# Expert loop of a decoder layer: token rows turned by VectorE in squares of 32 instead of by TensorE

## The chip, the cores and the metric

The kernel runs on one core of a Trainium2 chip. The metric is the device time of the program in microseconds (us). Times of whole runs are the median of three; the profile is of one more execution.

## The reference

One layer of a decoder: three attention groups on 512 tokens of width 1024, an output projection, and then the part that concerns us, a mixture of 32 experts with the four best experts for each token:

```
h = RMSNorm(x)
logits = h @ w_router + b_router            # 32 experts
top_v, top_e = top_k(logits, 4); gates = softmax(top_v)
for every expert e, on the tokens that chose it (padded blocks):
    gu   = h @ w_gate_up[e] + b_gate_up[e]  # 1024 -> 2048, gate = even, up = odd columns
    gate = min(gu[0::2], 7);  up = clip(gu[1::2], -7, 7)
    act  = (up + 1) * gate * sigmoid(1.702 * gate)
    y    = act @ w_down[e] + b_down[e]      # 1024 -> 1024
x = x + sum over the token's 4 experts of gate * y;  out = RMSNorm(x)
```

All inputs are float32, and all 32 experts' weights (12 MB each) are read from HBM.

## The kernel before, in words

The first 330 us or so compute the attention part, the router and a table that gives, for each block of up to 128 rows, the expert, the tokens and the gates. The rest is a loop over blocks. Here there are 33 blocks, 0 to 32: block 0 is done ahead of the loop, blocks 1 to 31 run through a loop body, and block 32 is the last, with a tail behind it.

**Arithmetic.** A float32 product is computed as three products of rounded parts: every operand is split into a high part (ScalarE, an `activation` copy to fp32r) and a low part (VectorE, the original minus the high part). `three` (lines 1296 to 1298) issues high x high, high x low and low x high into one PSUM bank.

**Weights.** A block needs twelve tiles of 1 MB: eight of gate and up (`gate_up`, rows k*128 to k*128+127 of the expert's matrix, 2048 columns) and four of down. SyncE loads each into one of six slots of `raw` (L448 and L455) once VectorE is done with the tile six before it. ScalarE makes the high part in one of four slots of `w_hi` (`hi`, L598) once TensorE has used the tile four before it (`half_used`); VectorE makes the low part in `w_lo` (`lo`, L859) once the high part is there; TensorE multiplies once the low part is there (`lo_ready`), twelve matmuls of 512 columns for each tile.

**Order within a block b.** It is written out by hand, engine by engine:

- TensorE (`one_block`): gate and up tiles 0 to 2, eight transposes of the previous block's activation (`turn_acts`, L1583), tiles 3 to 7, four bias matmuls (`gu_bias`, L1569), eight transposes of the next block's token rows (`turn_rows`, L1576), then the four down tiles of the previous block's activation.
- VectorE: low parts of tiles 4 to 6; the low parts of the turned activation in two halves (`turn_act`, L1174); low parts of tile 7 and of down tiles 0, 1 and 2; `clamp` (L1186, L1188); down tile 3; the low parts of the turned token rows in two halves (`turn_x`, L1169); `activate` (L1196); low parts of tiles 0 to 3 of the next block.
- ScalarE: the high parts in the same order, with the two turned operands (L751, L746), the sigmoid (L757) and the scaled output rows (`y_out`, L764) between them.
- GpSimd: an indirect DMA that gathers the next block's 128 token rows of 4 KB from `normed_rows` in HBM into `h_row` (`gather`, L539), four small DMAs for the biases (L571), and an indirect DMA that scatters the output rows (`scatter`, L564).

The eight transposes of `turn_rows` put token rows, features on the partitions, into PSUM banks 6 and 7; so do those of `turn_acts` for the activation. All of it is ordered by semaphores alone.

Of the kernel before, what the change touches and what calls it, by code (L numbers as in the profile page):

```python
# [10 lines left out]
I32 = mybir.dt.int32  # L11
# [37 lines left out]
N_CONST = C_FIRST + 2 * NT  # L49
# [16 lines left out]
def constants():  # L66
    c = np.zeros((P, N_CONST), np.float32)
    p = np.arange(P)
    c[:, C_IDENT:C_IDENT + P] = np.eye(P)
    c[:, C_TRI:C_TRI + P] = p[:, None] < p[None, :]  # L70
    c[:, C_ONES:C_ONES + P] = 1.0
    c[:, C_IOTA:C_IOTA + P] = p[None, :]
    for t in range(NT):
        c[:, C_TOK + t] = TOPK * (t * P + p) - NO_ROW
        c[:, C_FIRST + 2 * t] = t * P + p - NO_ROW
    c[:, C_ROWMOD] = p % E
    return c
# [14 lines left out]
def hymba_layer(nc, x, mem, attn_norm_g, mem_norm_g, w_in, diff_lambda_qk, diff_subln_g, w_mem_kv,  # L92
# [5 lines left out]
    h_dram = nc.dram_tensor("normed_rows", (S, D), F32).ap()  # L98
    y_dram = nc.dram_tensor("expert_rows", (TOPK * S, D), F32).ap()
# [11 lines left out]
    gu_dram = w_gate_up[0].rearrange("e (k p) n -> e p k n", p=P)  # L111
    dn_dram = w_down[0].rearrange("e (k p) n -> e p k n", p=P)

    with ExitStack() as ctx:
# [28 lines left out]
        exp_psum = psum[5][:, 2 * MAX_BLOCKS:3 * MAX_BLOCKS]  # L143
        pair_turn = turn_psum[:, :].rearrange("p (j s) -> p j s", j=2)
# [88 lines left out]
        gate_t, exp_f = (tabs[:, i, :] for i in (1, 2))  # L233
# [5 lines left out]
        idx_scatter = F[:, 15001:15002].bitcast(I32)  # L239

# [5 lines left out]
        last_tok = nrm[:, 0, 8:9]  # L246
        h_row = F[:, 4096:5120]
        act = F[:, 5120:6144]
# [44 lines left out]
        xtp_done, xhi_ready, xlo_ready = sem("xtp_done"), sem("xhi_ready"), sem("xlo_ready")  # L293
        atp_done, ahi_ready, alo_ready = sem("atp_done"), sem("ahi_ready"), sem("alo_ready")
# [126 lines left out]
        def _(sp):  # L421
# [22 lines left out]
            def gate_up(e, k, i, free=None):  # L444

                if free is not None:
                    sp.wait_ge(lo_ready, free)
                sp.dma_start(raw[:, i % 6, :].rearrange("p (e n) -> p e n", e=1),  # L448
                             gu_dram[bass.ds(e, 1), :, k, :]
                             .rearrange("e p n -> p e n")).then_inc(raw_in[i % 6], 16)  # L450
# [23 lines left out]
            with sp.Fori(1, loops + 1) as b:  # L474
                before, e = (sp.value_load(exp_i[0:1, bass.ds(b + i, 1)], min_val=0, max_val=E - 1)
                             for i in (-1, 0))
                for k in range(GU):
                    gate_up(e, k, GU + k, b * 12 + (7 + k))
                for j in range(DN):
                    down(before, j, 2 * GU + j, b * 12 + (7 + GU + j))  # L480
# [28 lines left out]
        def _(pool):  # L509
# [16 lines left out]
            for g in range(2):  # L526
                for i in range(2):
                    r0 = (2 * g + i) * E
                    pool.dma_start(bias_in[r0:r0 + E, :].rearrange("e (c n) -> e c n", c=2),
                                   b_gate_up[0].rearrange("e (c g n) -> g e c n", c=2, g=2)[g]).then_inc(bias_in_s, 16)  # L530
            pool.wait_ge(exp_ready, 1)
            loops = pool.value_load(loops_i[0:1, :], min_val=E - 1, max_val=MAX_LOOPS)

            def gather(column, n):
                n = n if isinstance(n, int) else pool.snap(n)
                pool.tensor_copy(idx_gather, tok_i[:, column]).then_inc(idx_ready, 1)  # L536
                pool.wait_ge(idx_ready, n)
                pool.sem_inc(gather_go, 1)
                pool.indirect_dma_start(h_row, None, h_dram,  # L539
                                        bass.IndirectOffsetOnAxis(idx_gather, 0),  # L540
                                        bounds_check=S - 1, oob_is_err=False).then_inc(h_in, 16)

            pool.wait_ge(tab_ready, 1)
            gather(slice(1, 2), 1)
# [28 lines left out]

            pool.wait_ge(bias_saved, 16)
# [5 lines left out]
            pool.wait_ge(xtp_done, loops + 1)  # L580
            bias_of_block(loops)
            scatter(loops - 1, loops * 2 + 1)
            pool.wait_ge(y_sent, loops * 16 + 32)
            pool.wait_ge(h_in, loops * 16)
# [3 lines left out]
        def _(a):  # L588
# [159 lines left out]

            def turn_act(q, n, into=ha):
# [19 lines left out]
            a.sem_inc(ahi_ready, 1)  # L769
# [20 lines left out]
            with a.Fori(1, loops) as b:  # L790
                for i in range(4, 7):
                    hi_m(GU + i, b)
                turn_act(0, b)
                turn_act(1, b)
                for i in range(7, 12):
                    hi_m(GU + i, b)
                sigmoid(b + 1)
                turn_x(0, b + 2)
                turn_x(1, b + 2)
                for i in range(12, 16):  # L800
                    hi_m(GU + i, b)
                y_out(b * 12 + (16 + GU), bass.ds(b - 1, 1), b * 16 + 16)
# [3 lines left out]
            turn_act(0, b)  # L806
            turn_act(1, b)
# [23 lines left out]
        def _(v):  # L831
# [306 lines left out]
            def read_table():  # L1138

                v.wait_ge(tab_in, 1)  # L1140
                link(v.tensor_scalar(y_row_i, tab_psum[:, 0:MAX_BLOCKS], float(NO_ROW), None, ALU.add))
                link(v.tensor_copy(gate_t, tab_psum[:, MAX_BLOCKS:2 * MAX_BLOCKS]))
                v.tensor_scalar(tok_i, y_row_i, 2, None, ALU.arith_shift_right).then_inc(tab_ready, 1)  # L1143
                v.wait_ge(tab_ready, 1)

# [21 lines left out]
            def turn_x(q, n, high=hx, low=lx):  # L1167
                v.wait_ge(xhi_ready, n)
                v.tensor_tensor(low[:, 4 * q:4 * q + 4, :], psum[6 + q][:, :].rearrange("p (k s) -> p k s", k=4),  # L1169
                                high[:, 4 * q:4 * q + 4, :].bitcast(F32), ALU.subtract).then_inc(xlo_ready, 1)  # L1170

# [38 lines left out]
            for i in range(4, GU):  # L1210
                lo_m(i)
            split_biases()
# [17 lines left out]
            with v.Fori(1, loops) as b:  # L1230
                for i in range(4, 7):
                    lo_m(GU + i, b)
                turn_act(0, b * 2)
                turn_act(1, b * 2 + 1)
                for i in range(7, 11):
                    lo_m(GU + i, b)
                clamp(b + 1)
                lo_m(GU + 11, b)
                turn_x(0, b * 2 + 3)
                turn_x(1, b * 2 + 4)  # L1240
                activate(b + 1, b)
                for i in range(12, 16):
                    lo_m(GU + i, b)
# [3 lines left out]
            turn_act(0, b * 2)  # L1247
            turn_act(1, b * 2 + 1)
# [7 lines left out]
            turn_act(0, b * 2 + 2, hx, lx)  # L1256
            turn_act(1, b * 2 + 3, hx, lx)
# [35 lines left out]
        def _(pe):  # L1293
# [243 lines left out]

            def half_in(i, b):
# [33 lines left out]
            def turn_rows(n_h):  # L1572

                pe.wait_ge(h_in, n_h)
                for k in range(KT):
                    ins = pe.transpose(psum[6 + k // 4][:, k % 4 * P:(k % 4 + 1) * P],  # L1576
                                       h_row[:, k * P:(k + 1) * P], ident)
                ins.then_inc(xtp_done, 1)
# [21 lines left out]
            for k in range(GU):  # L1600
                if k == 4:
                    pe.wait_ge(xlo_ready, 2)
                gate_up(k, k, None, (ha, la), (lambda: first_bias(0, gu_half)) if k == GU - 1 else None)
                if k == 1:
                    fill_table()
                if k == GU - 2:
                    turn_rows(16)
# [4 lines left out]
            def one_block(b, between=None):  # L1612

                pe.wait_ge(xlo_ready, b * 2 + 2)
# [5 lines left out]
                pe.wait_ge(alo_ready, b * 2)  # L1620
                turn_rows(b * 16 + 16)
# [11 lines left out]
            pe.wait_ge(xlo_ready, b * 2 + 2)  # L1633
# [5 lines left out]
            pe.wait_ge(alo_ready, b * 2)  # L1639
# [7 lines left out]
            for j in range(DN):  # L1647
                if j % 2 == 0:
                    pe.wait_ge(alo_ready, b * 2 + (1 + j // 2))
# [67 lines left out]
```

## Time and profile before

| what | value |
|---|---|
| median of 3 runs | 1495.49 us (1494.05 to 1495.63) |
| profiled execution, its time | 1496.8 us |
| its span, first to last instruction | 1495.1 us |
| TensorE busy | 1454.5 us (97%) |
| VectorE busy | 1297.5 us (87%) |
| ScalarE busy | 1016.3 us (68%) |
| GpSimd busy | 277.1 us (19%) |
| HBM read | 467.70 MB |

The span and the run's time differ by 1.7 us of start and end. A busy share over the whole span mixes the attention stage with the loop; the loop fills about three quarters of the span and is to be read by itself. Matmuls are pipelined: each is shown 390 ns long, but in the loop they start 226 ns apart.

### The profile page before, as it was taken

Reading aid. Unit: us, or ns where it says so; the run is one execution under the profiler, and the core shown is the slowest. Engines: PE = TensorE matmul, PEld = TensorE weight load, DVE = VectorE, ACT = ScalarE, POOL = GpSimd, SP = SyncE. Lnnn points to the kernel's source line nnn. Section 1 sums busy time; section 2 is a strip of 40 time slices with the busy share of each in tenths; the row PEclk is TensorE's granted clock in tenths of the full one; section 3 lists DMA queues with packets and bytes.
Section 4 is the critical chain, followed back from the end, with each engine's and each line's share of the span. In section 5 each row is a group of like instructions: output and inputs, shape, how many; then the busy total and the mean of one; then the engine's idle time right before and its main releaser. Section 6 shows DMA issues by size and latency. Waiting matters only on the chain.

```text
span 1495.1 us, 21387 instructions
## 1 busy us (share of the span) xinstructions
PE 1454.5 (97%) x7022; PEld 1188.0 (79%) x7022; DVE 1297.5 (87%) x1202; ACT 1016.3 (68%) x901; POOL 277.1 (19%) x282
## 2 busy tenths in 40 slices
PE   5999999899999999999999999999999999999996
PEld 5877877788888888888888888888888888888883
DVE  7258554799999999999999999999999999999998
ACT  5344344457777777777777777777777777777772
POOL 0000000032232222222222222222222222222210
PEclk9999989899999999999999999999999999999998
DMA  9411030289999999999999999999999999999994
GB/s 345 144 57 57 33 141 16 102 325 388 373 384 373 380 375 375 377 374 370 381 374 366 367 380 375 366 375 377 374 376 378 380 370 375 379 370 368 369 378 181
DMA packets 102335, 472.64 MB, mean 316 GB/s; under 512 B 16500, under 2 KB 16540, under 8 KB 68001
## 3 DMA queue, kind: packets, MB, share of 16 engines
q1 hardware_dynamic: 87632, 451.71, 77.4%
q0 software_dynamic: 14672, 20.53, 3.8%
q8 instruction: 18, 0.29, 0.1%
q14 instruction: 13, 0.10, 0.0%
HBM read 467.70 MB, written 22.02 MB: 328 GB/s over the span
## 4 chain that ended last, share of the span: by engine, by line
PE 94%; DVE 3%; DMA 1%; ACT 1%; issue 0%; SPq 0%; DVEq 0%
PE gu_bank L1296 17%; PE gu_bank L1298 17%; PE gu_bank L1297 17%; PE turn_bank L1296 8%; PE turn_bank L1298 8%; PE turn_bank L1297 8%; PE bank L1576 2%; PE bank L1583 2%; PE bank L1296 2%; PE bank L1486 2%; PE bank L1298 1%; PE bank L1297 1%; PE gu_bank L1432 1%; DMA arena<-in_x_dram 1%; PE turn_bank L1461 1%; PE gu_bank L1569 1%
## 5 line engine op out<-in xcount | busy, mean ns | idle before, releaser
L859 DVE TENSOR_TENSOR w_lo<-raw,w_hi 128x2048 fp32r<-128x2048 f32 x411 | 931.5, 2288 | 101.3 <-ACT w_hi L598 96.4
L598 ACT ACTIVATE w_hi<-raw 128x2048 fp32r<-128x2048 f32 x411 | 784.5, 1920 | 209.0 <-PE gu_bank L1298 178.5
L1296 PE MATMUL gu_bank<-w_hi,turned 128*128 128x512 f32 x1080 | 423.8, 392 | 1.1 <-ACT arena L781 1.1
L1298 PE MATMUL gu_bank<-w_hi,turned 128*128 128x512 f32 x1080 | 420.5, 389 | 0.0
L1297 PE MATMUL gu_bank<-w_lo,turned 128*128 128x512 f32 x1080 | 420.4, 389 | 0.0
L1296 PEld LDWEIGHTS gu_bank<-w_hi,turned 128*128 128x128 f32 x1080 | 202.8, 188 | 43.3 <-ACT arena L781 1.4
L1298 PEld LDWEIGHTS gu_bank<-w_hi,turned 128*128 128x128 f32 x1080 | 202.7, 188 | 42.3
L1297 PEld LDWEIGHTS gu_bank<-w_lo,turned 128*128 128x128 f32 x1080 | 202.9, 188 | 40.8
L1296 PE MATMUL turn_bank<-w_hi,turned 128*128 128x512 f32 (+1 forms) x544 | 213.4, 392 | 0.0
L1298 PE MATMUL turn_bank<-w_hi,turned 128*128 128x512 f32 (+1 forms) x544 | 210.4, 387 | 0.0
L1297 PE MATMUL turn_bank<-w_lo,turned 128*128 128x512 f32 (+1 forms) x544 | 210.3, 387 | 0.0
L564 POOL DMA_INDIRECT expert_rows<-arena x32 | 58.9, 1842 | 807.2 <-ACT arena L764 781.2
L1298 PEld LDWEIGHTS turn_bank<-w_hi,turned 128*128 128x128 f32 x544 | 102.2, 188 | 20.8
L1296 PEld LDWEIGHTS turn_bank<-w_hi,turned 128*128 128x128 f32 x544 | 102.4, 188 | 20.0 <-issue 0.2
L1297 PEld LDWEIGHTS turn_bank<-w_lo,turned 128*128 128x128 f32 x544 | 102.3, 188 | 19.6
L539 POOL DMA_INDIRECT arena<-normed_rows,arena x32 | 77.9, 2434 | 29.1 <-POOL arena L536 25.9
L757 ACT ACTIVATE arena<-gu_bank 128x1024 f32<-128x1024 f32 x32 | 32.9, 1029 | 65.4 <-DVE arena L1188 65.4
L571 POOL DMA_DIRECT2D turned<-split_biases x128 | 67.1, 550 | 2.0 <-issue 1.9
L707 ACT ACTIVATE raw<-turn_bank 128x512 f32<-128x512 f32 (+5 forms) x32 | 17.3, 542 | 52.1 <-PE turn_bank L1461 52.0
L536 POOL COPY arena<-arena 128x1 int32 (+1 forms) x32 | 46.3, 1445 | 7.0 <-DVE arena L1143 6.9
L723 ACT ACTIVATE arena<-arena,stat 128x128 f32<-128x128 f32 (+3 forms) x48 | 26.5, 554 | 24.3 <-DVE stat L936 24.3
L746 ACT ACTIVATE turned<-bank 128x512 fp32r<-128x512 f32 x66 | 35.7, 597 | 10.6 <-PE bank L1521 9.0
(290 smaller groups left out, 1375.4 us busy)
## 6 DMA issues: line engine op xcount, KB each, us to landing
raw<-in_w_gate_up_dram SPq DMA_DIRECT2D x264, 1024.0 KB, 7.9
raw<-in_w_down_dram SPq DMA_DIRECT2D x132, 1024.0 KB, 9.8
raw<-in_w_in_dram SPq DMA_DIRECT2D x10, 1024.0 KB, 7.8
raw<-in_w_out_dram SPq DMA_DIRECT2D x4, 1024.0 KB, 5.4
raw<-expert_rows SPq DMA_DIRECT2D x4, 1024.0 KB, 6.4
raw<-in_w_mem_kv_dram SPq DMA_DIRECT2D x2, 1024.0 KB, 12.2
arena<-in_x_dram SPq DMA_DIRECT2D x1, 2048.0 KB, 13.6
arena<-in_position_tables_dram SPq DMA_DIRECT2D x1, 2048.0 KB, 18.2
```

Source lines behind the costliest of these rows:

```text
L536: pool.tensor_copy(idx_gather, tok_i[:, column]).then_inc(idx_ready, 1)
L539: pool.indirect_dma_start(h_row, None, h_dram, bass.IndirectOffsetOnAxis(idx_gather, 0), bounds_check=S - 1, oob_is_err=False).then_inc(h_ ...
L564: pool.indirect_dma_start(y_dram, bass.IndirectOffsetOnAxis(idx_scatter, 0), y_row, None, bounds_check=TOPK * S - 1, oob_is_err=False).the ...
L571: pool.dma_start(bias_now[c * E:c * E + 2, :].unsqueeze(1), bias_rows[:, bass.ds(e, 1), c // 2, c % 2, :]).then_inc(bias_now_in, 16)
L598: a.activation(home, raw_ap, ACT.Copy).then_inc(hi_ready, 1)
L746: a.activation(into[:, 4 * q:4 * q + 4, :], psum[6 + q][:, :].rearrange("p (k s) -> p k s", k=4), ACT.Copy).then_inc(xhi_ready, 1)
L757: a.activation(sig_t, gu_psum[:, :].rearrange("p (i two) -> p two i", two=2)[:, 0, :], ACT.Sigmoid, scale=ALPHA).then_inc(sig_ready, 1)
L859: v.tensor_tensor(home[1], raw_ap, home[0].bitcast(F32), ALU.subtract).then_inc(lo_ready, 1)
L1296: pe.matmul(bank, a[0], b[0], start=first, stop=False)
L1297: pe.matmul(bank, a[0], b[1], start=False, stop=False)
L1298: return pe.matmul(bank, a[1], b[0], start=False, stop=last)
L1486: ins = pe.matmul(psum[BANK["pv", r]][:, j * DH:j * DH + width], pt[:, r % 2, j, kb * P:(kb + 1) * P], values[:, kb, v0:v0 + width], start ...
```

## The change

Token rows of blocks 2 and later are no longer transposed by TensorE. Each 4 KB row is seen as four quarters of 256 features. GpSimd issues four indirect DMAs, one for each group c of 32 tokens: partition 32a + s receives quarter a of token 32c + s, 1 KB. VectorE then turns squares of 32 by 32: feature 8s + k of a quarter lands on partition 32a + s, column k, so its input is read with a step of eight elements. For a tile k the partition p now holds feature 8p + k, and so the gate and up tiles are rows 8p + k of the matrix ("every eighth row") instead of rows 128k + p; block 0 keeps the old rows (`gu_first`). Index tables for the quarters are made once, ahead of the loop (`spread_tokens` on TensorE, `number_quarters` on VectorE, four copies on GpSimd). Block 1 still gets its rows by the old gather and TensorE, reading `h_row` with the step of eight. In the loop, the split into high and low parts is done in one instruction of 1024 columns for each operand and engine instead of two of 512. GpSimd's order changes: the gather for block b+2 goes out once VectorE has turned the rows of block b+1, and is followed by a wait on `gu_done`, the biases and the scatter.

```diff
-    gu_dram = w_gate_up[0].rearrange("e (k p) n -> e p k n", p=P)
+    gu_first = w_gate_up[0].rearrange("e (k p) n -> e p k n", p=P)
+    gu_dram = w_gate_up[0].rearrange("e (p k) n -> e p k n", p=P)
+    h_quarters = h_dram.rearrange("s (a n) -> (s a) n", a=4)
+        h_parts = h_row.rearrange("p (s k) -> p k s", k=KT)
+        h_turn = h_row.rearrange("p (c s k) -> p c k s", c=4, k=KT)
 # GpSimd
+            def gather_quarters(column, n):
+                pool.tensor_copy(idx_four, quarter_idx...[:, :, column]...).then_inc(idx_ready, 1)
+                pool.wait_ge(idx_ready, n)
+                for c in range(4):
+                    pool.indirect_dma_start(h_row[:, c * 256:(c + 1) * 256], None, h_quarters,
+                                            bass.IndirectOffsetOnAxis(idx_four[:, c:c + 1], 0), ...)
-            with pool.Fori(1, loops) as b:
-                pool.wait_ge(xtp_done, b + 1)
-                gather(bass.ds(b + 1, 1), b * 2 + 1)
-                bias_of_block(b)
-                scatter(b - 1, b * 2 + 2)
+            with pool.Fori(1, loops - 1) as b:
+                pool.wait_ge(rows_turned, b)
+                gather_quarters(bass.ds(b + 2, 1), b * 2 + 2)
+                pool.wait_ge(gu_done, b + 1)
+                bias_of_block(b + 1)
+                scatter(b - 1, b * 2 + 3)
 # VectorE
+            def turn_rows(n_h, split):
+                v.wait_ge(h_in, n_h)
+                v.wait_ge(alo_ready, split)
+                for c in range(4):
+                    ins = v.transpose(turned_eight[:, :, c * Q:(c + 1) * Q], h_turn[:, c])
+                ins.then_inc(rows_turned, 1)
             with v.Fori(1, loops) as b:
                 for i in range(4, 7):
                     lo_m(GU + i, b)
-                turn_act(0, b * 2)
-                turn_act(1, b * 2 + 1)
-                for i in range(7, 11):
+                split_act(b)
+                for i in range(7, 10):
                     lo_m(GU + i, b)
+                turn_rows(b * 64 + 16, b)
+                lo_m(GU + 10, b)
                 clamp(b + 1)
                 lo_m(GU + 11, b)
-                turn_x(0, b * 2 + 3)
-                turn_x(1, b * 2 + 4)
+                split_rows(b + 4)
                 activate(b + 1, b)
 # ScalarE: two halves -> one piece, for rows and for the activation
-                turn_act(0, b)
-                turn_act(1, b)
+                split_act(b)
-                turn_x(0, b + 2)
-                turn_x(1, b + 2)
+                split_rows(b)
 # TensorE, one_block
                 gu_bias(b)
-                pe.wait_ge(alo_ready, b * 2)
-                turn_rows(b * 16 + 16)
+                pe.wait_ge(alo_ready, b)
```

## Rows read from the trace of the kernel before

**Rows 1.** Span and granted TensorE clock of the core.
```profile
core 0: 1495.1 us, clock 0.987
```
**Rows 2.** Stages: engines' busy us, granted clock, DMA share, GB/s.
```profile
20.00:30.00 10.00, 7.13 (x47) 6.93 (x47) 9.39 (x20) 5.15 (x6) 0.00 (x0) 0.83 1.05 387
358.50:1444.00 1085.50, 1085.50 (x5080) 892.37 (x5079) 1021.06 (x590) 831.09 (x589) 249.97 (x246) 1.00 0.95 375
```
**Rows 3.** One block, same columns (PE, PEld, DVE, ACT, POOL).
```profile
707.25:742.28 35.03, 35.03 (x165) 28.80 (x165) 32.95 (x21) 26.81 (x20) 8.04 (x8) 1.00 0.96 379
```
**Rows 4.** VectorE's second clamp instruction: duration min/median/max, first and last start.
```profile
L1188 DVE SCALAR_TENSOR_TENSOR arena<-gu_bank,arena x32: 1223/1224/1226, 358.5 to 1444.0; 128x1024 f32<-128x1024 f32 x32
```
**Rows 5.** Waits, 500 to 1400 us: total, times, longest.
```profile
ACT w_hi L598 <- PE gu_bank L1298: 135.0, 179, 0.8
DVE w_lo L859 <- ACT w_hi L598: 48.1, 127, 0.4
```
**Rows 6.** Timeline of TensorE about the row transposes (start us, us).
```profile
705.38 0.39 PE L1298 MATMUL gu_bank<-w_hi,turned 128*128 128x512 f32 x1
705.70 0.51 PE L1569 MATMUL gu_bank<-turned 2*128 2x512 f32 x4
706.14 1.09 PE L1576 MATMUL bank<-cst,arena 128*128 128x128 f32 x8
706.99 0.48 PE L1296 MATMUL turn_bank<-w_hi,turned 128*128 128x512 f32 x1
```
**Rows 7.** Timeline of TensorE about the activation's transposes.
```profile
691.12 1.03 PE L1583 MATMUL bank<-cst,arena 128*128 128x128 f32 x8
691.91 0.48 PE L1296 MATMUL gu_bank<-w_hi,turned 128*128 128x512 f32 x1
```
**Rows 8.** Timeline of VectorE and ScalarE in the same block.
```profile
700.37 1.92 ACT L598 ACTIVATE w_hi<-raw 128x2048 fp32r<-128x2048 f32 x1 [0.80 <-PE gu_bank L1298]
702.32 2.29 DVE L859 TENSOR_TENSOR w_lo<-raw,w_hi 128x2048 fp32r<-128x2048 f32 x1 [0.43 <-ACT w_hi L598]
705.04 2.29 DVE L859 TENSOR_TENSOR w_lo<-raw,w_hi 128x2048 fp32r<-128x2048 f32 x1 [0.43 <-ACT w_hi L598]
707.25 1.22 DVE L1186 TENSOR_SCALAR arena<-gu_bank 128x1024 f32<-128x1024 f32 x1
709.64 2.28 DVE L859 TENSOR_TENSOR w_lo<-raw,w_hi 128x2048 fp32r<-128x2048 f32 x1
709.76 1.03 ACT L757 ACTIVATE arena<-gu_bank 128x1024 f32<-128x1024 f32 x1 [2.04 <-DVE arena L1188]
711.84 1.28 DVE L1169 TENSOR_TENSOR turned<-bank,turned 128x512 fp32r<-128x512 f32 x2
713.04 1.21 DVE L1196 SCALAR_TENSOR_TENSOR arena<-arena 128x1024 f32<-128x1024 f32 x1
714.18 11.21 DVE L859 TENSOR_TENSOR w_lo<-raw,w_hi 128x2048 fp32r<-128x2048 f32 x5
```
**Rows 9.** VectorE groups by line and shape: busy us, mean ns.
```profile
L1111 DVE TENSOR_REDUCE arena<-arena 128x16 f32<-128x512 f32 x1 | 0.7, 686 | 0.0
L1260 DVE TENSOR_REDUCE arena<-arena 128x128 f32<-128x512 f32 x1 | 1.1, 1126 | 0.0
L1014 DVE TENSOR_REDUCE arena<-arena 128x96 f32<-128x384 f32 x1 | 0.8, 835 | 0.0
L1014 DVE TENSOR_REDUCE arena<-arena 128x32 f32<-128x128 f32 x1 | 0.4, 367 | 0.0
L1064 DVE TENSOR_TENSOR arena<-arena,gains 128x256 f32<-128x256 f32 x1 | 0.4, 415 | 0.0
```
**Rows 10.** GpSimd's indirect gather: duration ns min/median/max.
```profile
L539 POOL DMA_INDIRECT arena<-normed_rows,arena x32: 2168/2467/2483, 317.2 to 1391.8; - x32
```
**Rows 11.** DMA issues: KB each, median us from issue to landing.
```profile
raw<-in_w_gate_up_dram SPq DMA_DIRECT2D x264, 1024.0 KB, 7.9
...
arena<-normed_rows,arena POOLq DMA_INDIRECT x32, 8.9
```

More of the change, by code:

```diff
@@ L48 @@
 C_FIRST = C_ROWMOD + 1
-N_CONST = C_FIRST + 2 * NT
+C_QUARTER = C_FIRST + 2 * NT
+N_CONST = C_QUARTER + 1
+Q = P // 4
 def position_tables():
@@ L76, in constants @@
     c[:, C_ROWMOD] = p % E
+    c[:, C_QUARTER] = p // Q
     return c
@@ L143, in hymba_layer @@
         exp_psum = psum[5][:, 2 * MAX_BLOCKS:3 * MAX_BLOCKS]
+        spread_psum = psum[5][:, 3 * MAX_BLOCKS:7 * MAX_BLOCKS]
+        turned_eight = end_psum[:, :].rearrange("p (k s) -> p k s", k=KT)
         pair_turn = turn_psum[:, :].rearrange("p (j s) -> p j s", j=2)
@@ L232, in hymba_layer @@
         tabs = F[:, 14592:14592 + 8 * MAX_BLOCKS].rearrange("p (i b) -> p i b", i=8)
-        gate_t, exp_f = (tabs[:, i, :] for i in (1, 2))
+        tok_f, gate_t, exp_f = (tabs[:, i, :] for i in range(3))
         y_row_i = tabs[:, 4, :].bitcast(I32)
@@ L239, in hymba_layer @@
         idx_scatter = F[:, 15001:15002].bitcast(I32)
+        idx_four = F[:, 15002:15006].bitcast(I32)
+        quarter_idx = F[:, 15104:15104 + 4 * MAX_BLOCKS].bitcast(I32)
         bias_in = F[:, 6144:6144 + FF]
@@ L293, in hymba_layer @@
         xtp_done, xhi_ready, xlo_ready = sem("xtp_done"), sem("xhi_ready"), sem("xlo_ready")
+        spread_ready, rows_turned, tok_ready, spread_in, quarters_ready = (
+            sem(n) for n in ("spread_ready", "rows_turned", "tok_ready", "spread_in", "quarters_ready"))
         atp_done, ahi_ready, alo_ready = sem("atp_done"), sem("ahi_ready"), sem("alo_ready")
@@ L442, in _, with gate_up @@
             sp.dma_start(F[:, 0:2 * D].rearrange("p (t d) -> p t d", t=2), x_rows[:, 2:4, :]).then_inc(x_again[1], 16)
-            def gate_up(e, k, i, free=None):
+            def gate_up(e, k, i, free=None, rows=gu_first):
                 if free is not None:
@@ L448, in gate_up @@
                 sp.dma_start(raw[:, i % 6, :].rearrange("p (e n) -> p e n", e=1),
-                             gu_dram[bass.ds(e, 1), :, k, :]
+                             rows[bass.ds(e, 1), :, k, :]
                              .rearrange("e p n -> p e n")).then_inc(raw_in[i % 6], 16)
@@ L572, in bias_of_block @@
                                    bias_rows[:, bass.ds(e, 1), c // 2, c % 2, :]).then_inc(bias_now_in, 16)
+            pool.wait_ge(xtp_done, 2)
+            pool.wait_ge(quarters_ready, 1)
+            gather_quarters(slice(2, 3), 3)
             pool.wait_ge(bias_saved, 16)
-            with pool.Fori(1, loops) as b:
-                pool.wait_ge(xtp_done, b + 1)
-                gather(bass.ds(b + 1, 1), b * 2 + 1)
-                bias_of_block(b)
-                scatter(b - 1, b * 2 + 2)
-            pool.wait_ge(xtp_done, loops + 1)
+            bias_of_block(1)
+            with pool.Fori(1, loops - 1) as b:
[4 more added lines that the diff above has]
+                scatter(b - 1, b * 2 + 3)
+            pool.wait_ge(gu_done, loops)
             bias_of_block(loops)
+            scatter(loops - 2, loops * 2)
             scatter(loops - 1, loops * 2 + 1)
             pool.wait_ge(y_sent, loops * 16 + 32)
-            pool.wait_ge(h_in, loops * 16)
         @block.scalar
@@ L747, in turn_x, with split_rows, split_act @@
                              psum[6 + q][:, :].rearrange("p (k s) -> p k s", k=4), ACT.Copy).then_inc(xhi_ready, 1)
+            def split_rows(n):
+                a.wait_ge(rows_turned, n)
+                a.activation(hx, turned_eight, ACT.Copy).then_inc(xhi_ready, 1)
+            def split_act(n):
+                a.wait_ge(atp_done, n)
+                a.activation(ha, turned_eight, ACT.Copy).then_inc(ahi_ready, 1)
             def turn_act(q, n, into=ha):
@@ L1144, in read_table, with number_quarters @@
                 v.wait_ge(tab_ready, 1)
+                v.tensor_copy(tok_f, tok_i).then_inc(tok_ready, 1)
+            def number_quarters():
+                v.wait_ge(spread_in, 1)
+                v.tensor_scalar(quarter_idx, spread_psum, 4.0, cst[:, C_QUARTER:C_QUARTER + 1], ALU.mult,
+                                ALU.add).then_inc(quarters_ready, 1)
             def number_blocks():
@@ L1170, in turn_x, with split_rows, split_act @@
                                 high[:, 4 * q:4 * q + 4, :].bitcast(F32), ALU.subtract).then_inc(xlo_ready, 1)
+            def turn_rows(n_h, split):
+                v.wait_ge(h_in, n_h)
+                v.wait_ge(alo_ready, split)
+                for c in range(4):
+                    ins = v.transpose(turned_eight[:, :, c * Q:(c + 1) * Q],
+                                      h_turn[:, c])
+                ins.then_inc(rows_turned, 1)
+            def split_rows(n):
+                v.wait_ge(xhi_ready, n)
+                v.tensor_tensor(lx, turned_eight, hx.bitcast(F32), ALU.subtract).then_inc(xlo_ready, 1)
+            def split_act(n):
+                v.wait_ge(ahi_ready, n)
+                v.tensor_tensor(la, turned_eight, ha.bitcast(F32), ALU.subtract).then_inc(alo_ready, 1)
             def turn_act(q, n, high=ha, low=la):
@@ L1211, in _ @@
                 lo_m(i)
+            number_quarters()
             split_biases()
@@ L1536, in fill_table, with spread_tokens @@
                 ins.then_inc(tab_in, 1)
+            def spread_tokens():
+                pe.wait_ge(spread_ready, 4)
+                pe.wait_ge(tok_ready, 1)
+                for c in range(4):
+                    ins = pe.matmul(spread_psum[:, c * MAX_BLOCKS:(c + 1) * MAX_BLOCKS], spread[:, c * P:(c + 1) * P], tok_f,
+                                    start=True, stop=True)
+                ins.then_inc(spread_in, 1)
             def half_in(i, b):
@@ L1570, in gu_bias, with turn_first_rows @@
                 ins.then_inc(gu_done, 1)
-            def turn_rows(n_h):
-                pe.wait_ge(h_in, n_h)
+            def turn_first_rows():
+                pe.wait_ge(h_in, 16)
                 for k in range(KT):
-                    ins = pe.transpose(psum[6 + k // 4][:, k % 4 * P:(k % 4 + 1) * P],
-                                       h_row[:, k * P:(k + 1) * P], ident)
+                    ins = pe.transpose(psum[6 + k // 4][:, k % 4 * P:(k % 4 + 1) * P], h_parts[:, k], ident)
                 ins.then_inc(xtp_done, 1)
@@ L1605, in _ @@
                     fill_table()
+                if k == 4:
+                    spread_tokens()
                 if k == GU - 2:
-                    turn_rows(16)
+                    turn_first_rows()
             first_bias(1, gu_done)
```

38 lines of the change are left out of this document (20 added, 18 removed).

## The prediction

> **What bounds the kernel now.** I read the core's span first [rows 1]: the profiled execution took 1496.8 us with a span of 1495.1; the median of the runs is 1495.5, so what I sum for this execution I lower by 1.3. Next the stages [rows 2]: from 358.5 to 1444.0 TensorE is busy all the time at a granted clock of 1.00 (the 2.4 GHz level), VectorE 1021.1 of 1085.5 us (94%), ScalarE 77%, the DMA share is 0.95. Two clamps 31 blocks apart start at 358.5 and 1444.0 [rows 4], so a block takes 1085.5/31 = 35.02 us; one block by itself shows 35.03, with VectorE busy 32.95 [rows 3]. The waits [rows 5] point one way: VectorE waits for ScalarE (48 us), ScalarE for TensorE (135 us), and nobody in the loop for a weight DMA. So TensorE sets the pace, but VectorE has only 2.1 us of air in each block, and the change takes work from the one and gives it to the other.
>
> TensorE's block: a tile of 12 matmuls takes 2.72 us (in step with it VectorE's low parts start at 702.32 and 705.04 [rows 8]), so a matmul starts every 0.2265 us, and the block's 144 are 32.62 us. What is left, 2.41 us, is bias, row transposes, activation transposes and the slower first matmuls behind them.
>
> **TensorE's part.** It loses eight transposes in each of blocks 1 to 31. They start at 706.14 and the next matmul starts at 706.99 [rows 6]: 0.85 us. It can't be under 0.8 (the activation's eight, with no bias ahead, take 691.91 - 691.12 = 0.79 [rows 7]), nor over 0.94: from the matmul at 705.38 to the one at 706.99 are 1.61 us, of which 0.23 is the ordinary step and 0.44 the bias matmuls (705.70 to 706.14). TensorE's own floor becomes 35.03 - 0.85 = 34.2 us a block (34.1 to 34.25): 31 x 0.85 = 26 us is the most that the change can bring.
>
> **VectorE's part.** Removed: one instruction boundary in each of two splits. Two halves of 512 take 1.28 us together [rows 8], one of 1024 takes 1.22 (the clamp's instructions [rows 4, 8]): 0.06 each, 0.1 us a block. Added: four transposes of 256 elements for each partition, read with a step of 32 bytes. No row shows a VectorE transpose. From below: an instruction of 256 elements at full rate takes 0.415 us [rows 9]; back to back the next starts about 0.08 before the end (two of 512 take 1.28 together, one 0.68), so 0.34 each, 1.4 us in all. From above, for reads with a wide step: reductions that read with a step of 128 bytes took 0.367 for 128 elements, 0.835 for 384 and 1.126 for 512, against 0.686 for 512 read in order [rows 9]. A line from 0.367 to 0.835 gives 0.60 for 256, one from 0.367 to 1.126 gives 0.62; two whole cycles an element in place of one would be 0.415 + 256/0.96 ns = 0.68 (the row of 2048 elements in 2.29 us against that of 1024 in 1.22 [rows 8] gives 0.96 elements a ns). Less the overlap: 0.52 to 0.60 each, 2.1 to 2.4 us in all. Nothing excludes that the transpose itself runs at half of either rate: 4.4 us is the far end. I take 2.2, by the rows with the wide step, because the transposes' reads step through memory as those do and the in-order rows do not.
>
> The Trainium skill has a rule that speaks against the change: in SBUF — State Buffer, Door 1: The DMA port swizzle, SBUF is read in lines of 16 bytes and each access that moves to a new line pays. The reductions agree with it (1.126 against 0.686); by it 32 bytes are as bad as 128. Its page VectorE: DVE Perf Modes, The three transpose paths, speaks for the change: a VectorE transpose of 128 x 128 bf16 in 311 ns, nothing slower than an ordinary instruction. An estimate by that page alone, 311 ns + 128/0.96 ns = 0.44 each, is 1.5 us for four and a faster kernel. No run here shows a transpose yet.
>
> **What that does to a block.** VectorE's busy time becomes 32.95 - 0.1 + 2.2 = 35.05: by its sum alone it is over TensorE's 34.2. But order matters too, since the weights' slots let VectorE run only so far ahead. Follow the ring of waits round one block:
>
> - VectorE from the start of the low part of down tile 1: that tile 2.21 (705.04 to 707.25), four transposes T, down tile 2 2.21, clamp 2.39 (707.25 to 709.64), down tile 3 2.20, rows' split 1.13, activate 1.14 (713.04 to 714.18), low part of the next block's tile 0 2.29 [rows 8]. Sum 13.57 + T.
> - TensorE, released by it: 0.1 to its first matmul, six tiles 16.31, the activation's transposes with the slower matmul behind them 0.79 + 0.09 (the first of a group is 0.48 long instead of 0.39 [rows 7]), 0.16 to the end of the last matmul. Sum 17.45.
> - ScalarE makes the high part in the slot that tile 5 frees: 0.04 + 1.92 + 0.03 [rows 8] = 1.99, and VectorE is back at down tile 1.
>
> Round: 33.0 + T. With T = 2.2 it is 35.2; with T = 1.4, 34.4. The ring binds from T = 1.2, and the kernel breaks even at T = 2.0, that is 0.50 us a transpose. As the waits go: TensorE should wait for VectorE at the next block's tile 0, ScalarE for the clamp well over the 2.04 of now [rows 8]. I add 0.1 for semaphore steps that the sum rounds off: 35.3 against 35.02, 31 blocks x 0.3 = +9 us. Between the ends of T: 34.4 gives 31 x -0.6 = -18 us, 35.5 gives +15.
>
> **The edits at nothing, and what hides them.** GpSimd: four gathers of 2.47 [rows 10] in place of one, 9.9 us, with an index copy ahead. They go out when VectorE has turned the block before, and are wanted 35 us later; with landing (8.9 us [rows 11]) there are some 14 us of air. Behind them on GpSimd's queue stand the biases, wanted only 25 us on, and the scatter, which can't go before ScalarE's output rows at the block's end anyway. If that cover were gone, VectorE would stand at the transposes; I see no way to that but a gather of over 5 us. The first such gather, beside block 1, starts late and has to land within about 25 us; at worst a few us once. ScalarE's splits lose 0.1 us of an engine with 8 us of air, but in one piece the rows' split has to end before VectorE's (the sigmoid takes 1.03 for 1024 elements [rows 8], the split as much, together the 2.2 of down tile 3: just so). Before the loop: four small matmuls, at most 0.9, a VectorE copy and a scale, 0.2 each: +1 us, once.
>
> The weights: a tile is now 128 rows of 8 KB, 64 KB apart, in place of 1 MB in one piece. The loads of the first stage are 2 KB pieces 10 KB apart and ran at 387 GB/s [rows 2], and the loop needs 1.05 MB in 2.72 us, 386. A gate and up tile lands after 7.9 us [rows 11] in a slot freed some 12 us before it is wanted. I cost it at nothing. A row pitch in a power of two has a warning in the Trainium skill (DMA: Bandwidth & Descriptors, Latency and other measured facts: from 2 MiB on copies slow down, at 512 KiB hardly); by it 64 KB is harmless, and no run here shows it. The gather's 512 packets of 1 KB instead of 128 of 4 KB load the DMA engines a little more; at a share of 0.95 that is where a cost could hide, under 1 us a block.
>
> Sum: 1496.8 + 9 + 1 = 1507 for the profiled execution, about 1505.5 for a median.
>
> **The rivals.**
>
> 1. *The transposes run at full rate* (T = 1.4 to 1.6). For it: the clamp reads with a step of 8 bytes at full rate, 1.22 us for 1024 elements [rows 8]; nothing in the loop reads with 32. Against it: the reductions. The block becomes 34.4 to 34.6: -13 to -18 us, 1478 to 1483. If T also slipped under 1.2, TensorE's floor gives 1469.
> 2. *Transpose or chain dearer than that*: T from 2.8 to 4.4, for instance if the 4-byte squares take two passes, or stalls about the split in one piece. From T = 2.0 each us more is a us a block: 1523 to 1573.
> 3. *The strided weights are slow.* From 2.9 us a tile the DMA engines, not VectorE, would set the block. At 300 GB/s eight tiles take 3.5: 8 x 0.8 = 6 us a block, some +190 us. Against it: 387 GB/s with 10 KB pitch.
> 4. *It all comes out even*: T near 2.0. Nothing singles that value out but its place in the middle.
>
> **How the numbers follow.** Slower by the strided read, the forecast: 38%. Full rate: 35%. Dearer transposes: 13%. Slow weights: 4%. Even: 10%. Within 0.2% is 3 us on either side, about what a measurement of this kernel can tell from no change. Of the forecast's case a twentieth of the whole falls within 3 us, of rival 1 nearly nothing: faster 0.36, same 0.12, slower 0.52. The likeliest case's own range is 1499 to 1515. The range for 8 in 10 reaches down into rival 1, to 1476, and up into rival 2, to 1528.
>
> **What would show it.** In the profile of the changed kernel: four VectorE transposes a block, 0.6 us each (0.42 would be rival 1, over 0.8 rival 2); block period from clamp to clamp 35.3; TensorE no longer 100% busy in the loop, with a wait for VectorE's low part at a block's first tile; ScalarE's wait for the clamp 3.5 us or more; VectorE's waits for ScalarE nearly gone; no wait for a weight DMA or for the gather. The prediction is wrong if the transposes are under 0.5 us each, or if a queue that I costed at nothing shows up in the waits.

## The result, and the profile after

| | median us | ratio to before (95% interval) |
|---|---|---|
| kernel before | 1494.8 | |
| changed kernel | 1512.8 (1509.6 to 1515.1) | 1.0117 (1.0102 to 1.0132) |

The change makes the kernel 18 us slower; the forecast was 1505.5 us, range 1476 to 1528, with a chance of 0.52 for slower. The profiled execution took 1509.6 us, its span is 1508.0.

The stage from 358.5 to 1444.0 of the changed kernel (columns as in [rows 2]):

```profile
358.50:1444.00 1085.50, 1058.85 (x4781) 855.48 (x4781) 1059.54 (x640) 811.82 (x523) 435.53 (x334) 1.00 0.95 368
```

TensorE, at 1085.5 in [rows 2], now shows 27 us without work, and VectorE has gone from 94% to 98%. The waits from 500 to 1400 us, as in [rows 5]:

```profile
ACT w_hi L626 <- PE gu_bank L1358: 129.8, 175, 0.8
ACT arena L795 <- DVE arena L1248: 98.0, 26, 3.8
...
PEld gu_bank L1356 <- DVE w_lo L893: 34.1, 26, 1.3
...
PE gu_bank L1356 <- DVE w_lo L893: 23.1, 26, 0.9
...
DVE w_lo L893 <- ACT w_hi L626: 18.6, 50, 0.4
```

Once in each of 26 blocks TensorE waits for a low part: its weight load starts 1.3 us late, and its matmuls (modelled ends) show a gap of 0.9. The new instructions among VectorE's groups (behind the bar: busy us, then mean ns of one), and the part of one block on VectorE's timeline where the transposes stand:

```profile
L1218 DVE STREAM_TRANSPOSE bank<-arena 128x256 f32<-128x256 f32 x100 | 59.3, 663 | 0.0
```
```profile
706.73 2.29 DVE L893 TENSOR_TENSOR w_lo<-raw,w_hi 128x2048 fp32r<-128x2048 f32 x1 [0.43 <-ACT w_hi L626]
708.94 2.36 DVE L1218 STREAM_TRANSPOSE bank<-arena 128x256 f32<-128x256 f32 x4
711.20 2.27 DVE L893 TENSOR_TENSOR w_lo<-raw,w_hi 128x2048 fp32r<-128x2048 f32 x1
713.39 1.21 DVE L1246 TENSOR_SCALAR arena<-gu_bank 128x1024 f32<-128x1024 f32 x1
714.64 1.23 DVE L1248 SCALAR_TENSOR_TENSOR arena<-gu_bank,arena 128x1024 f32<-128x1024 f32 x1
```

From one clamp start (678.00) to the next (713.39) are 35.39 us; [rows 3] has 35.03. The chain of waits that ended last shows the ring of the prediction step by step, here one turn of it (start us, us):

```profile
704.51 0.24 PE gu_bank L1358
704.78 1.93 ACT w_hi L626
707.08 1.86 issue
708.94 0.56 DVE bank L1218
709.54 1.76 DVE bank L1218 x3
711.30 2.18 DVE w_lo L893
713.48 1.14 DVE arena L1246
714.81 0.97 issue
715.78 2.14 DVE w_lo L893
718.02 1.20 DVE turned L1225
719.23 0.50 DVE arena L1256
719.73 0.55 issue
720.28 2.29 DVE w_lo L893
722.62 0.50 PE gu_bank L1356
```

Read it down: the last matmul of gate and up tile 5 frees a slot (704.5), ScalarE fills it, VectorE makes down tile 1's low part, turns the rows, goes on through the clamp, the splits and the activation, and TensorE starts tile 0 at 722.6, 0.05 us after the low part is there. "Issue" lines are gaps in what the profile could link. All three lie inside VectorE's own run: the first one here is the low part that starts at 706.73 in the timeline above.

**Where the 18 us are.** Clamp starts mark the stages, in both profiles:

| stretch | before | after | difference |
|---|---|---|---|
| start to the block table read by VectorE | 313.17 | 307.42 | -5.8 |
| table to clamp of block 1 | 45.29 | 49.64 | +4.3 |
| to clamp of block 2 | 34.84 | 38.66 | +3.8 |
| 29 blocks to clamp of block 31 | 29 x 35.02 | 29 x 35.43 | +11.8 |
| last block | 35.02 | 33.66 | -1.4 |
| tail | 51.1 | 51.2 | +0.1 |

The first row is not the change: ahead of the table the two kernels do nearly the same, but from 200 to 240 us the granted clock was 0.83 in the profile of before and 0.96 in that after. Other profiles with the change bear this out: in the runs "Transposes earlier" and "Order and place together" below that clock was 0.83 too, and the table was read at 312.9 and 313.3. Without this row the sum is 18.7, near the 18.0 between the medians. About 10.4 are in the blocks from 3 on and 8 are paid once.

Behind part of the 8 us stand two waits before block 1's clamp; then come ten us of the stages and the six in which TensorE works again (columns as in [rows 2]):

```profile
PE gu_bank L1638 <- DMA turned<-split_biases: 3.2, 1, 3.2
...
DVE bank L1218 <- DMA arena<-normed_rows,arena: 1.3, 1, 1.3
```
```profile
350.00:360.00 10.00, 6.78 (x21) 4.72 (x20) 8.70 (x9) 3.60 (x3) 4.61 (x4) 0.68 1.01 404
354.00:360.00 6.00, 6.00 (x17) 4.40 (x18) 5.96 (x4) 1.69 (x2) 4.50 (x4) 0.50 1.00 401
```

TensorE waits for block 1's biases. GpSimd's timeline shows why: the first four gathers run from 336.8 to 346.7 us, and the biases leave behind them.

```profile
343.68 3.03 POOL L559 DMA_INDIRECT arena<-normed_rows,arena  x1 [0.31 <-issue]
346.71 2.15 POOL L594 DMA_DIRECT2D turned<-split_biases  x4
```

Behind the wait TensorE works at a granted clock of 0.50 (the 1.2 GHz level) until 360.4 us; its matmuls start 0.43 us apart there, and 0.23 before the wait and after 360.7.

### The profile page after: what moved, and what is told of

It is laid out like the page before. It is cut to its first block, busy times and chain, and to the rows that moved or that the text cites. A ratio compares the mean times of both kernels' runs of the same rounds, so it can differ in the third digit from the quotient of the medians.

```text
span 1508.0 us, 21053 instructions
## 1 busy us (share of the span) xinstructions
PE 1437.2 (95%) x6782; PEld 1158.3 (77%) x6782; DVE 1351.5 (90%) x1265; ACT 1005.5 (67%) x838; POOL 474.5 (31%) x379
## 4 chain that ended last, share of the span: by engine, by line
PE 57%; DVE 27%; issue 9%; ACT 4%; DMA 1%; POOL 1%; DVEq 0%; SPq 0%; POOLq 0%; ACTq 0%
PE gu_bank L1356 14%; DVE w_lo L893 14%; PE gu_bank L1358 13%; PE gu_bank L1357 13%; DVE bank L1218 5%; ACT w_hi L626 4%; DVE turned L1225 2%; DVE arena L1246 2%; PE bank L1651 2%; PE bank L1356 2%; PE bank L1358 1%; PE bank L1357 1%; PE bank L1546 1%; PE gu_bank L1492 1%; PE turn_bank L1356 1%
## 5 line engine op out<-in xcount | busy, mean ns | idle before, releaser
L554 POOL COPY arena<-arena 128x4 int32 (+1 forms) x31 | 62.7, 2024 | 494.1 <-DVE bank L1218 494.1
L559 POOL DMA_INDIRECT arena<-normed_rows,arena x124 | 186.7, 1506 | 59.8 <-issue 33.1
L587 POOL DMA_INDIRECT expert_rows<-arena x32 | 91.0, 2845 | 102.7 <-ACT arena L802 100.6
L1218 DVE STREAM_TRANSPOSE bank<-arena 128x256 f32<-128x256 f32 x124 | 73.3, 662 | 1.3 <-DMA arena<-normed_rows,arena 1.3
```

Of the source, the lines that this page charges most:

```text
L554: pool.tensor_copy(idx_four, quarter_idx.rearrange("p (c b) -> p c b", c=4)[:, :, column] .rearrange("p c b -> p (c b)")).then_inc(idx_rea ...
L559: pool.indirect_dma_start(h_row[:, c * 256:(c + 1) * 256], None, h_quarters, bass.IndirectOffsetOnAxis(idx_four[:, c:c + 1], 0), bounds_ch ...
L587: pool.indirect_dma_start(y_dram, bass.IndirectOffsetOnAxis(idx_scatter, 0), y_row, None, bounds_check=TOPK * S - 1, oob_is_err=False).the ...
L1218: ins = v.transpose(turned_eight[:, :, c * Q:(c + 1) * Q], h_turn[:, c])
```

## The experiments

All times are medians of their own runs. The experiments were measured in three sets, each with its own runs of the kernel before (medians 1494.6, 1495.9 and 1495.0 us); the ratios are to that. "Block" is the distance of clamps in the steady loop.

**Reads in order.** One line:

```diff
-        h_turn = h_row.rearrange("p (c s k) -> p c k s", c=4, k=KT)
+        h_turn = h_row.rearrange("p (c k s) -> p c k s", c=4, k=KT)
```

> The changed kernel with one line different: the four transposes read their 256 elements in order (c k s) instead of with a step of 32 bytes (c s k). The weights stay at every eighth row, so rows and weights no longer match and the output is not the layer's. My theory (the step makes the reads slow): one transpose falls from 0.66 us to 0.42-0.45, the four from 2.26 to 1.5; the ring of waits gives 33.0 + 1.5 = 34.5 us a block instead of 35.4; the run is 26 us (24 to 30) under the changed kernel, near 1486. Rival (turning squares of 4-byte elements is itself slow, whatever the reads): transposes stay at 0.66 us, block 35.4, run near 1513.

Measured: 1483.6 us, ratio 0.9931 (0.9909 to 0.9954), block 34.50. The transposes and the time of four:

```profile
L1218 DVE STREAM_TRANSPOSE bank<-arena x124: 416/418/460, 354.2 to 1394.1; 128x256 f32<-128x256 f32 x124
```
```profile
703.25 1.43 DVE L1218 STREAM_TRANSPOSE bank<-arena 128x256 f32<-128x256 f32 x4
704.59 2.27 DVE L893 TENSOR_TENSOR w_lo<-raw,w_hi 128x2048 fp32r<-128x2048 f32 x1
```

0.66 us becomes 0.42, four take 1.34 in place of 2.26, and the block falls by 0.93: slope one, as the ring says. The square of 4-byte elements has no price of its own, since 0.418 us is what an ordinary instruction of 256 elements takes (0.415 [rows 9]); the step of 32 bytes has. That alone turns a loss of 18 us into a gain of 11.

**No transposes.** The body of VectorE's `turn_rows` behind its waits becomes `v.sem_inc(rows_turned, 1)`.

> The changed kernel with the four transposes left out (VectorE only signals that it has done them); gathers, weights, splits stay. Rows of blocks 2 on are whatever the PSUM banks hold, so the output is not the layer's. My theory (only the transposes hold the block over TensorE's floor): block 34.2 us (34.1 to 34.3), TensorE 100% busy in the loop again, run near 1475. Rival (four gathers, 1 KB packets or strided weights cost something that VectorE covers now): block at 34.5 or more, with waits for a DMA or GpSimd in the loop, run over 1483.

Measured: 1477.0 us, 0.9884 (0.9862 to 0.9905), block 34.24 (bias matmuls at 702.55 and 736.79), TensorE 1085.4 of 1085.5 us busy. No wait for a weight DMA or GpSimd from 500 to 1400 us. So the strided tiles, the 1 KB gathers and the splits hold nothing up there, and 34.24 is TensorE's floor.

**Old rows of the weights.** The loop's call of `gate_up` without `gu_dram`.

> The changed kernel, gate and up tiles in the loop again 128 neighbouring rows (1 MB in one piece) instead of every eighth row; the rows are turned for the other order, so the output is not the layer's. My theory (strided tiles cost nothing): block 35.4 us, run 1513 +- 3, tile landing within 0.5 us of 7.5. Rival (the 64 KB pitch costs DMA time, seen as late landing): block under 35.2 or a start (blocks 1 and 2) quicker by 2 us or more, run under 1509.

Measured: 1512.7 us, 1.0129 (1.0110 to 1.0148), block 35.43, blocks 1 and 2 as in the changed kernel (clamps at 357.4 and 396.0). The 64 KB pitch costs the run nothing, as forecast. But the landing was not within 0.5 us of 7.5. The DMA issues (KB each, median us from issue to landing) of the changed kernel, then of this one:

```profile
raw<-in_w_gate_up_dram SPq DMA_DIRECT2D x264, 1024.0 KB, 7.5
```
```profile
raw<-in_w_gate_up_dram SPq DMA_DIRECT2D x264, 1024.0 KB, 5.1
```

The strided tiles may land about 2 us later, then, with nobody waiting for them. It is not shown: the other kernels with strided tiles of 1 MB whose profiles give this median show 6.2 to 7.7, though none as little as 5.1.

**Transposes earlier.**

```diff
                 split_act(b)
-                for i in range(7, 10):
-                    lo_m(GU + i, b)
                 turn_rows(b * 64 + 16, b)
+                lo_m(GU + 7, b)
+                lo_m(GU + 8, b)
+                lo_m(GU + 9, b)
                 lo_m(GU + 10, b)
```

> The changed kernel with the four transposes moved in VectorE's order from before the low part of down tile 2 to directly behind the activation's split, before tile 7; same work, right output. My theory (a ring of waits from down tile 1 over TensorE's tiles 0-5 sets the block): the transposes leave that ring, which falls to 33.2, and what is left is VectorE's own sum, 35.0 to 35.15: block 0.25-0.4 us shorter, run 8-12 us under the changed kernel, near 1503, VectorE over 99% busy in the loop, its waits for ScalarE (18.6 us between 500 and 1400) gone. Rival (VectorE's sum alone already sets the block): no change, 35.4.

Measured: 1493.1 us, 0.9991 (0.9981 to 1.0001), block 34.65. The direction is the ring's, but 0.78 us a block is two to three times what I expected, and the run is 20 us under the changed kernel instead of 8 to 12.

```profile
358.50:1444.00 1085.50, 1082.41 (x4882) 874.19 (x4883) 1079.73 (x655) 825.85 (x531) 470.95 (x336) 1.00 0.98 378
```

VectorE (the third number behind the comma) is busy 1079.7 of 1085.5 us, and from 500 to 1400 us no wait of VectorE is listed, so 34.65 is its own sum for a block, not the 35.05 that I had worked out. The changed kernel agrees: its block of 35.43 less VectorE's waits for ScalarE (18.6 us in 900, 0.73 a block) is 34.70. In this place the transposes wait 4.6 us for the first gather, and block 1's clamp comes at 365.9.

**First gather sooner.** GpSimd, ahead of the loop:

```diff
             pool.dma_start(bias_dram, bias).then_inc(bias_saved, 16)
+            pool.wait_ge(xtp_done, 2)
+            pool.wait_ge(quarters_ready, 1)
+            gather_quarters(slice(2, 3), 2)
             pool.tensor_copy(idx_scatter, ...)
-            pool.wait_ge(idx_ready, 2)
+            pool.wait_ge(idx_ready, 3)
...
             pool.indirect_dma_start(y_dram, ...)      # zero rows, waits for ScalarE
-            pool.wait_ge(xtp_done, 2)
-            pool.wait_ge(quarters_ready, 1)
-            gather_quarters(slice(2, 3), 3)
             pool.wait_ge(bias_saved, 16)
```

> The changed kernel with only GpSimd's order ahead of the loop changed: the first four gathers go out before the scatter of zero rows, not behind it (which waits for ScalarE), so block 1's biases leave GpSimd earlier. Right output. My theory (the changed kernel loses 7 to 8 us once, about block 1: TensorE waits 3.2 us for block 1's biases that stand behind the four gathers, VectorE 1.3 us for the gather, and TensorE's clock drops behind the wait): both waits gone, clamp 1 comes 4 us sooner after the table, block 2 takes 35.5-36 instead of 38.7 us; steady block still 35.4; run 6-8 us under the changed kernel, near 1506. Rival (the start is slow because the weight DMAs run at their limit there): the waits go but clamp 1 and 2 stay within 1 us, run 1511 or more.

Measured: 1509.9 us, 1.0103 (1.0082 to 1.0123). The block stays at 35.43. Both waits are gone and the ten us read

```profile
350.00:360.00 10.00, 10.00 (x47) 7.81 (x46) 9.97 (x9) 4.86 (x3) 2.62 (x2) 1.00 1.04 421
```

Table to clamp 1 is 48.45 us (from 49.64), block 2 35.48 (from 38.66): 4.4 us in the profile and 4.0 by the medians (14.0 us over the kernel before instead of 18.0), where I expected 6 to 8. Clamp 1 came only 1.2 us sooner, not 4: the clamp lost only the 1.3 us of VectorE's wait, and block 2 lost the rest. The 3.2 us between 48.45 and the 45.29 of before are not waits of GpSimd's making. VectorE's timelines, in which it hardly stands still in either kernel, account for them: block 1's transposes add 2.3, the index table and a copy 0.3, and a wait for TensorE in block 0 that was not there before 0.6.

**Both orders.** Right output, the change's layout kept.

> The changed kernel with both orders changed: transposes directly behind the activation's split, and the first gathers ahead of the zero scatter. Right output. Theory: the two gains add: steady block 34.65 us as with the early transposes alone, no wait for the first gather (4.6 us there) or biases; 1493 less 7-8 us = near 1485, 8-10 us under the kernel before. Rival (the start costs come back as another wait): 1490 or more.

Measured: 1484.0 us, 0.9923 (0.9899 to 0.9946), block 34.65, and neither wait is left. This is the fastest kernel with right output here: 12 us under the one before, where the changed one is 18 over it.

**All three, with reads in order and matching weights.** Rows 256a + 32k + s don't lie at one step over the partitions, so each tile went in four DMAs of 32 partitions:

```diff
-                sp.dma_start(raw[:, i % 6, :]..., rows[bass.ds(e, 1), :, k, :]...)
+                for a in range(4):
+                    sp.dma_start(raw[a * Q:(a + 1) * Q, i % 6, :]..., rows[bass.ds(e, 1), a, :, k, :]...)
```

> Right output with the transposes reading in order: gate and up tiles are loaded as rows 256a + 32k + s, each tile (and each down tile) by four DMAs of 32 partitions, the transposes directly behind the activation's split, the first gathers ahead of the zero scatter, and block 1's rows put in order by one VectorE copy ahead of the loop. Theory: ring 33.2 and VectorE's sum 34.65 - 0.9 = 33.75 both lie under TensorE's floor, so the block is 34.2-34.3 us and nothing in the start waits: 1477 (the kernel without transposes) less 6 = near 1471, 23 us under the kernel before. Rival (four DMAs of 256 KB a tile, 1.3 us of SyncE's issue each, or the DMA engines at a share of 0.97 bind): VectorE or ScalarE wait for weight DMAs, block 34.6 or more, run over 1480.

Measured: 2251.7 us, 1.508 (1.503 to 1.512). My theory fell here: what came is the rival's sign, ScalarE waiting for weight DMAs, with a time far beyond the 1480 us that the rival named. Waits and DMA from 500 to 1400 us (the last two numbers of the second fence's line are DMA share and GB/s):

```profile
DVE w_lo L895 <- ACT w_hi L628: 354.7, 167, 4.7
ACT w_hi L628 <- DMA raw<-in_w_gate_up_dram: 282.6, 127, 3.1
...
ACT w_hi L628 <- DMA raw<-in_w_down_dram: 191.7, 60, 5.1
```
```profile
500.00:1400.00 900.00, 634.99 (x2449) 458.82 (x2450) 541.64 (x330) 421.28 (x267) 210.93 (x168) 0.94 1.02 231
```

The DMA engines are busy all the time at 231 GB/s. The next two runs ask why.

**Four DMAs a tile, by columns.** The kernel with both orders, with `for c in range(4)` over 512 columns in both loads.

> The kernel with early transposes and early first gathers (strided reads, right output), each weight tile cut into four DMAs by columns (128 partitions x 2 KB), where the slow kernel cut them by partitions (32 partitions x 8 KB): as many DMAs of 256 KB, but each reaches all partitions. In the slow kernel the DMA engines were busy all the time at 231 GB/s, against 375 before. Theory (a DMA into 32 neighbouring partitions gets only half of the ways into SBUF): 370 GB/s or more, block under 35, run 1484 to 1495. Rival (many DMAs of 256 KB are slow in themselves): near 231 GB/s again, run over 2000.

Measured: 1489.7 us, 0.9971 (0.9960 to 0.9983):

```profile
500.00:1400.00 900.00, 893.74 (x4039) 722.02 (x4038) 894.11 (x544) 687.03 (x440) 446.92 (x285) 1.00 1.04 377
```

As many DMAs of the same size, with packets of 2 KB instead of 8 KB or 4 KB, and 377 GB/s. So neither the count nor the size of the DMAs is the cause. What is left is how few partitions each one writes. Each DMA's source differs too (gate and up: 256 KB in one piece of HBM, here pieces of 2 KB), which no run separates; but the kernel before reads 1 MB in one piece at 375 GB/s [rows 2]. The four DMAs by columns are not free either: 5.3 us under the kernel before instead of 12, blocks of 34.76 on average, and ScalarE waits for weight DMAs in the loop (110 us of 900).

**Partition pieces in the order 0, 2, 1, 3.** `for a in (0, 2, 1, 3)`.

> The slow kernel with the four partition pieces of each tile issued in the order 0, 2, 1, 3 instead of 0, 1, 2, 3. Right output, reads in order. Theory of the halves (partitions 0 to 63 share one half of the ways, 64 to 127 the other): neighbouring DMAs in the queue now lie in different halves and overlap in part, rate between 231 and 375 GB/s, run between 1500 and 2000. If each DMA of 32 partitions is slow by itself, whatever its neighbour: 231 GB/s and 2250 again.

Measured: 2118.5 us, 1.416 (1.408 to 1.425), 247 GB/s. The time lies above the range that I gave for the theory of the halves and below the 2250 of its rival. The order matters, then, by 7% of the rate; that it does so through two halves of the partitions is not shown, and why neighbours in the queue overlap so little stays open. The Trainium skill (SBUF — State Buffer, Door 1: The DMA port swizzle) has partitions 0 to 31, and 0 to 63 too, on the same 8 of 16 ports; 231 beside 377 GB/s agrees with pieces that reach half of them; the 247 in the other order settles nothing.

**Order and place together, weights unchanged.**

> The changed kernel with both the reads in order (weights unchanged, so rows and weights don't match and the output is not the layer's) and the transposes directly behind the activation's split. Theory: ring at 33.2 and VectorE's sum at 34.65 - 0.9 = 33.75 are both under TensorE's floor: block 34.24 as in the kernel without transposes, run 1477 + the 3 us that the wait for the first gather costs more here, near 1480. Rival (4 transposes have a price besides their time): block 34.4 or more.

Measured: 1480.7 us, 0.9898 (0.9876 to 0.9921), block 34.23, TensorE busy 900.00 of 900 us between 500 and 1400. That is the floor of the kernel without transposes, with the transposes in. The wait for the first gather is 6.4 us here.

**The split in one piece, alone, on the kernel before.**

> The kernel before, with only the splits of the loop's turned operands made in one instruction of 1024 columns instead of two of 512 on ScalarE and VectorE. Right output. Theory: VectorE's busy time falls by 0.1 us a block, but TensorE sets the pace: block 35.03, run 1495 +- 2. Rival (the split in one piece comes later and holds TensorE or VectorE at the next block's first tile): block over 35.1, run over 1498.

Measured: 1494.3 us, 0.999 (0.9979 to 1.0000), block 35.03, VectorE busy 1017.0 of 1085.5 in place of 1021.1: 0.13 us a block, all of it hidden.

## Why the prediction was right, and where its sizes were off

- **TensorE's part**, 0.85 us a block, floor 34.2: 34.24 measured without transposes and 34.23 with hidden ones, so the eight transposes were worth 0.79. Right.
- **T, the four transposes**: I took 2.2, measured 2.26. The choice between the ends was the whole forecast, and by my own chances (38% against 35%) nearly an even bet. The reduction rows [rows 9] turned out to be the right neighbours: 0.60 to 0.62 for 256 elements by them, 0.66 measured; 0.415 for reads in order, 0.418 measured. That was in part luck: those reductions are another instruction, with a step of 128 bytes, and the slow ones also sum 4 elements to a result where the one read in order sums 32. Only the run with reads in order shows that the step is what costs here. The Trainium skill's rule of 16-byte lines (SBUF — State Buffer, Door 1: The DMA port swizzle) agrees with both steps (1126 ns against 686 with 128 bytes, 0.66 us against 0.418 with 32). The 311 ns that the Trainium skill (VectorE: DVE Perf Modes, The three transpose paths) gives for 128 x 128 bf16 fit reads in order: 0.44 us by the prediction's estimate, 0.418 measured.
- **The ring**, 33.0 + T + 0.1: with T = 2.26 it gives 35.36, measured 35.43 over 29 blocks. With T = 1.34 it gives 34.44, measured 34.50. The early transposes show it too: the same work elsewhere in the order is 0.78 us a block less. The signs at TensorE's tile 0 and at the clamp (ScalarE waits 3.8 us) came as forecast.
- **VectorE's sum** for a block, 35.05, was mis-sized: 34.65. I took the 32.95 us of busy time of one block [rows 3] as work. But a low part that starts after a wait takes 2.29, and one that follows another adds 2.20 (15.4 us for seven), so busy time in a loop with waits overstates what the engine needs. It misled the expectation for the early transposes, not the forecast, since the ring lies above it. The sign that VectorE's waits for ScalarE would be nearly gone failed for the same reason: 0.73 us a block are left, the room between 34.65 and the ring.
- **The edits at nothing.** Strided tiles, small packets, splits, gathers in the steady loop: nothing in time, as said. By its last sign the prediction is wrong in one place all the same, since a queue that it costed at nothing shows up in the waits. What failed is the sentence that the biases behind the gathers are "wanted only 25 us on". True in the loop, false for block 1, where the first four gathers start behind ScalarE's zero rows and end 3 us too late for the biases. TensorE waits 3.2 us, runs at a lower clock behind it, and block 2 is 3.8 us longer than before. With the moved gather 4.4 us of this went. The rest of the 8 us paid once is 3.2 in the start, most of it block 1's own transposes, which had no room in VectorE's order there, and 0.6 in block 2; I had put +1. Seven of the 8 us between the forecast's +10 and the measured +18 are this, the rest is the steady block. The ring brought the forecast near; the term for the start was off by a factor of eight.
- The rivals: full rate was the right price for the wrong read (1478 to 1483 forecast, 1483.6 measured once the reads were in order). Strided weights cost no time in the run.

## What to carry to other kernels

When work goes from the engine that sets the pace to one that is 94% busy, don't stop at the sum of busy times: follow the ring of waits with its slots once round, because the place in the order decided as much here (0.78 us a block) as the work that TensorE was saved (0.79). A cost at nothing in the steady loop has to be checked again for the first turn, where queues start late. And a layout that makes reads step through memory should be priced from rows that read so, even of another instruction if there are no others, and then checked by a run with one line changed, as the reads in order were here.

## What the runs showed of the hardware

- A VectorE transpose in squares of 32 of 256 float32 elements, SBUF to PSUM, takes 0.418 us read in order and 0.66 us with a step of 32 bytes: 0.24 us more for 256 elements, at the 0.96 elements a ns of the prediction nearly an element's time more for each.
- DMAs that each write only 32 neighbouring partitions brought 231 GB/s with the DMA engines busy all the time (share 1.02), 247 in the order 0, 2, 1, 3; tiles in as many DMAs over 128 partitions 377.
- Gate and up rows 64 KB apart, 8 KB each, do at this pace as well as 1 MB in one piece: blocks of 35.43 us in both, 369 GB/s in both; the median landing was 7.5 and 5.1 us.
- Behind a wait of 3.2 us TensorE's granted clock was 0.50 from 354 to 360 us, and its matmuls started 0.43 us apart instead of 0.23; without the wait the clock stayed 1.00.
- Indirect gathers of 128 pieces of 1 KB took GpSimd 1.5 us each on average in the loop (1.0 to 2.0), not the 2.47 of one with 4 KB rows [rows 10].
